# Second norm and router woven into the output products of a decoder step, tile by tile, in one block with the experts; first gather in full fp32 rows

## What is computed

```python
def merge_branches(x, o_a, o_b, g_mrg, w_up_a, w_up_b, w_out):
    g_a, g_b = jnp.split(g_mrg, 2, axis=-1)
    return x + (g_a * (o_a @ w_up_a) + g_b * (o_b @ w_up_b)) @ w_out

def moe_ffn(x, norm_ffn, w_router, b_router, w_gu, b_gu, w_down, b_down):
    xn = rms_norm(x, norm_ffn)
    logits = (xn @ w_router).astype(jnp.float32) + b_router.astype(jnp.float32)
    top_v, top_e = lax.top_k(logits, TOP_K)        # 4 of 32 experts
    gates = jax.nn.softmax(top_v, axis=-1)
    ...
        h = xn[tok] @ w_gu[e] + b_gu[e]
        gate = jnp.minimum(h[:, :D_FF], SWIGLU_LIMIT)
        up = jnp.clip(h[:, D_FF:], -SWIGLU_LIMIT, SWIGLU_LIMIT)
        return ((up + 1.0) * gate * jax.nn.sigmoid(SWIGLU_ALPHA * gate)) @ w_down[e] + b_down[e]
    ...
    return x + out
```

## Time and profile before

| | us |
|---|---|
| median of 3 runs | 1383.79 (1383.48 to 1386.16) |
| the profiled execution | 1390.39 |
| its span, first to last instruction | 1388.6 |
| PE busy | 1255.2 (90%) |
| DVE busy | 355.3 (26%) |
| ACT busy | 218.5 (16%) |
| POOL busy | 24.0 (2%) |
| DMA, mean over the span | 333 GB/s |

### The profile page before, as it was taken

The page is one execution under the profiler, slowest core; times in us unless marked ns, Lnnn a source line. Parts: engine busy times, 40 slices in busy tenths (PEclk is TensorE's granted clock), DMA queues, the critical chain, the costliest instruction groups (busy, mean ns, idle before and its releaser), DMA issues.

```text
span 1388.6 us, 17391 instructions
## 1 busy us (share of the span) xinstructions
PE 1255.2 (90%) x6724; PEld 590.2 (43%) x6724; DVE 355.3 (26%) x905; ACT 218.5 (16%) x476; POOL 24.0 (2%) x26
## 2 busy tenths in 40 slices
PE   6998999999458999999988989889898998989987
PEld 3546678866143343443333323323243333333323
DVE  1551445514254121221211212112121111202113
ACT  2222124410131011011000101001110001010010
POOL 0000000002020000000000000000000000000000
PEclk9999999999757999999999999999999999999999
DMA  9546641487304978999999999999999999999994
GB/s 337 171 119 184 227 152 47 101 278 278 136 4 194 411 292 350 427 429 427 429 428 429 428 429 428 428 429 429 428 428 429 429 428 428 429 429 428 428 429 174
DMA packets 74896, 462.05 MB, mean 333 GB/s; under 512 B 18036, under 2 KB 32996, under 8 KB 50020
## 3 DMA queue, kind: packets, MB, share of 16 engines
q1 hardware_dynamic: 74852, 461.45, 82.1%
HBM read 458.46 MB, written 5.07 MB: 334 GB/s over the span
## 4 chain that ended last, share of the span: by engine, by line
DMA 44%; PE 24%; ACT 1%; DVE 0%; issue 0%; SPq 0%; DVEq 0%; ACTq 0%
DMA arena<-w_down 44%; PE banks L1607 11%; PE banks L1572 9%; PE banks L1553 1%; PE banks L1524 1%; PE banks L1535 0%; PE banks L1563 0%; ACT arena L1633 0%; DVE arena L1958 0%; PE banks L1527 0%; ACT arena L1648 0%; PE banks L1600 0%; PE banks L1585 0%; SPq L424 0%; DVE arena L1685 0%
## 5 line engine op out<-in xcount | busy, mean ns | idle before, releaser
L1572 PE MATMUL banks<-arena 128*64 128x512 f32 x2112 | 472.7, 597 | 37.7 <-DMA arena<-w_gu 37.7
L1572 PEld LDWEIGHTS banks<-arena 128*64 128x64 f32 x2112 | 147.8, 137 | 336.0 <-issue 254.3
L1607 PE MATMUL banks<-arena 128*64 128x512 f32 x1056 | 237.7, 594 | 17.8 <-DMA arena<-w_down 17.8
L1662 DVE TENSOR_SCALAR arena<-banks 128x512 f32<-128x512 f32 x33 | 22.8, 692 | 518.1 <-PE banks L1572 518.1
L1607 PEld LDWEIGHTS banks<-arena 128*64 128x64 f32 x1056 | 72.7, 136 | 164.4 <-issue 118.3
L1637 ACT ACTIVATE arena<-arena 128x512 f32<-128x512 f32 x33 | 20.8, 630 | 559.3 <-DVE arena L1662 559.3
L1685 DVE TENSOR_TENSOR arena<-banks,arena 128x528 f32<-128x528 f32 x68 | 48.1, 708 | 173.6 <-PE banks L1553 173.6
L1143 PE MATMUL banks<-arena 128*128 128x512 f32 (+1 forms) x192 | 80.5, 579 | 0.0
L1553 PE MATMUL banks<-arena 128*128 128x264 f32 x272 | 65.1, 391 | 2.5 <-ACT arena L1648 1.3
L605 PE MATMUL banks<-arena 128*128 128x264 f32 x256 | 62.2, 398 | 0.5 <-ACT arena L832 0.5
L1553 PEld LDWEIGHTS banks<-arena 128*128 128x128 f32 x272 | 50.0, 189 | 23.8 <-issue 12.2
(11 more groups left out here) (330 smaller groups left out, 918.5 us busy)
## 6 DMA issues: line engine op xcount, KB each, us to landing
arena<-w_gu SPq DMA_DIRECT2D x128, 2048.0 KB, 24.9
arena<-w_down SPq DMA_DIRECT2D x64, 2048.0 KB, 25.2
arena<-w_in SPq DMA_DIRECT2D x9, 2048.0 KB, 12.2
arena<-cache_moba_k SPq DMA_DIRECT2D x16, 256.0 KB, 2.8
arena<-cache_moba_v SPq DMA_DIRECT2D x16, 256.0 KB, 2.8
arena<-w_out SPq DMA_DIRECT2D x2, 2048.0 KB, 13.3
arena<-cmp_w_k SPq DMA_DIRECT2D x1, 2048.0 KB, 8.6
arena<-cmp_w_v SPq DMA_DIRECT2D x1, 2048.0 KB, 15.1
```

What stands on the lines that cost most here:

```text
L1572: mm = nc.tensor.matmul(banks[64 * x:64 * x + 64, BG + b, :], xgT[:, c % 4, 64 * (c // 4):64 * (c // 4) + 64], w[:, D * b + 512 * x:D * b ...
L1607: mm = nc.tensor.matmul(banks[64 * x:64 * x + 64, BY, :], aT[:, c, 64 * part:64 * part + 64], w[:, 512 * x:512 * x + 512], start=False, st ...
L1662: nc.vector.tensor_scalar(gate, banks[:, BG, :], LIMIT, None, ALU.min).then_inc(S["clip"], 1)
```

## The change

1. The blocks of the norm and of the router are gone; all of it stands in the dense block, and the experts' programs follow in the same block with no barrier (`experts_sp`, `experts_pe`, `experts_act`, `experts_dve`, otherwise the old code).
2. `route_pe`, `route_act` and `route_dve` take the place of the output products' code. The sample rows come first, then four half tiles of 512 columns. Once a half tile is added, its rows are transposed as they are, not normed. The gain is folded into w_router (one multiplication, with the gain loaded one element per row), and the factor 1/rms is applied to the logits. The second half of tile 1 is interrupted half way by the router products of tile 0.
3. Root by tile; the scaled rows are made on ScalarE beside this. The bias splits stand between VectorE's additions. w_router, b_router and the two forms of the gain are loaded behind the first expert's slots 0 and 1. Slots 3 and 5 wait for `out_done` 5.
4. `gather_first`: the first pass gathers from the fp32 rows themselves, 3 tiles by 2 halves, and doesn't wait for the three parts. The parts are made later: ScalarE casts, VectorE subtracts (`less`), POOL no longer.
5. The list products and the turn of the table stand inside gate_up of pass 0, after a quarter, a half and three quarters (`lists`). VectorE does the softmax weights, both `less`, `lists` and the table by expert before the clip of pass 0; before, `lists` came after its product.

```diff
+            sp.dma_start(gain2, t["norm_ffn"].partition_broadcast(P)).then_inc(r_in, 16)
+            sp.dma_start(w_router, t["w_router"].rearrange("(c p) n -> p c n", p=P)).then_inc(r_in, 16)
+            sp.dma_start(b_router, t["b_router"].partition_broadcast(P)).then_inc(r_in, 16)
+            with nc.allow_non_contiguous_dma("one gain per row of the router's weights"):
+                sp.dma_start(gainT, t["norm_ffn"].rearrange("(c p) -> p c", p=P)).then_inc(r_in, 16)
...
-            sp.wait_ge(out_done, 3)
+            sp.wait_ge(out_done, 5)
...
+            pe.wait_ge(S["sel"], 1)
+            pe.wait_ge(r_scaled, NT)
+            for i in range(NT):
+                r = ROWS[i]
+                for x in range(2):
+                    mm = nc.tensor.matmul(banks[64 * x:64 * x + 64, BX, :], sel_rows[0:r, i, :], xn2[0:r, i, 512 * x:512 * x + 512],
+                                          start=(i == 0), stop=(i == NT - 1), tile_position=(0, 64 * x))
+            mm.then_inc(S["gathered"], 1)
...
+            def turn_h(i, chunks, bank, done, turn):
+                r = ROWS[i]
+                pe.wait_ge(h_done, done)
+                for k, c in enumerate(chunks):
+                    mm = nc.tensor.transpose(banks[:, bank, r * k:r * k + r], h[0:r, i, P * c:P * c + P], ident[0:r, 0:r])
+                mm.then_inc(h_turned, 1)
...
+            def route(i, bank, chunks, kept):
+                r = ROWS[i]
+                pe.wait_ge(h_kept, kept)
+                for c in chunks:
+                    mm = nc.tensor.matmul(banks[0:r, bank, 0:NEXP], hT[:, c, P * i:P * i + r], w_router[:, c, :], start=(c == 0), stop=(c == KC - 1))
...
+            out_half(0, 0)
+            turn_h(2, range(KC), 5, 1, 1)
+            out_half(0, 1)
+            out_half(1, 0)
+            turn_h(0, range(4), 6, 2, 2)
+            turn_h(0, range(4, KC), 7, 3, 3)
+            pe.wait_ge(r_folded, 1)
+            route(2, 4, range(KC), 1)
+            turn_h(1, range(4), 5, 4, 4)
+            out_half(1, 1, lambda: route(0, 6, range(KC), 3))
+            route(1, 7, range(4), 4)
+            turn_h(1, range(4, KC), 0, 5, 5)
+            route(1, 7, range(4, KC), 5)
+            pe.wait_ge(r_chosen, 3)
...
+            square(3, 1, slice(512, D), 5)
+            act.wait_ge(r_mean, 1)
+            root(1, 3, h_mean)
+            keep_turned(1, range(4, KC), 0, 5)
+            scale(1, 3)
+            act.wait_ge(r_shifted, 1)
+            nc.scalar.activation(exps, exps, ACT.Exp).then_inc(r_exp, 1)
+            act.wait_ge(r_scaled, 3)
+            nc.scalar.copy(x_parts[:, 1, 0, :], xn2[:, 1, :]).then_inc(r_cast, 1)
...
+                dve.wait_ge(r_logits, k)
+                settle(nc.vector.scalar_tensor_tensor(logits[0:r, i, :], banks[0:r, bank, 0:NEXP], h_inv[0:r, i:i + 1], b_router[0:r, :], ALU.mult, ALU.add))
+                settle(nc.vector.max(top8[0:r, i, :], logits[0:r, i, :]))
+                settle(nc.vector.max_index(top_i[0:r, i, :], top8[0:r, i, :], logits[0:r, i, :]))
+                settle(nc.vector.tensor_copy(top_f[0:r, i, :], top_i[0:r, i, :]))
+                settle(nc.vector.tensor_tensor(hits[0:r], const("iota")[0:r, 0:NEXP].unsqueeze(1).broadcast_to([r, TOPK, NEXP]),
+                                               top_f[0:r, i, 0:TOPK].unsqueeze(2).broadcast_to([r, TOPK, NEXP]), ALU.is_equal))
+                nc.vector.tensor_reduce(chosen[0:r, i, :], hits[0:r].rearrange("p k e -> p e k"), X, ALU.add).then_inc(r_chosen, 1)
...
+            dve.wait_ge(r_in, 64)
+            nc.vector.tensor_tensor(w_router, w_router, gainT.unsqueeze(2).broadcast_to([P, KC, NEXP]), ALU.mult).then_inc(r_folded, 1)
             dve.wait_ge(h_in, 32)
+            dve.wait_ge(out_done, 1)
...
+            split_bias(0)
+            add_out(0, 0, 2)
+            dve.wait_ge(r_clear, 4)
+            gained(2, slice(0, D), 1).then_inc(r_gained, 1)
+            split_bias(1)
+            add_out(0, 1, 3)
+            invert(2, 1)
+            gained(0, slice(0, D), 3).then_inc(r_gained, 1)
+            invert(0, 2)
+            add_out(1, 0, 4)
+            dve.wait_ge(r_sq, 3)
+            nc.vector.tensor_scalar(h_mean, h_ss[:, 2:3], 1.0 / D, EPS, ALU.mult, ALU.add).then_inc(r_mean, 1)
+            choose(2, 4, 1)
+            gained(1, slice(0, 512), 4)
+            choose(0, 6, 2)
+            add_out(1, 1, 5)
+            gained(1, slice(512, D), 5).then_inc(r_gained, 1)
+            invert(1, 3)
+            choose(1, 7, 3)
+            nc.vector.tensor_tensor(exps, logits, top8[:, :, 0:1].broadcast_to([P, NT, NEXP]), ALU.subtract).then_inc(r_shifted, 1)
+            flat = rank.rearrange("p a b -> p (a b)")
+            dve.wait_ge(r_ranked, 1)
+            settle(nc.vector.scalar_tensor_tensor(flat, banks[:, 1, 0:NT * NEXP], 1.0, chosen.rearrange("p a b -> p (a b)"), ALU.add, ALU.mult))
+            settle(nc.vector.tensor_scalar(flat, flat, -1.0, None, ALU.add))
...
+            def lists(c):
+                if c == 1:
+                    pe.wait_ge(l_wanted, 1)
+                    nc.tensor.matmul(banks[:, 7, 0:1], const("before"), over[:, 1:2], start=True, stop=True).then_inc(l_found, 1)
+                if c == 3:
+                    pe.wait_ge(l_wanted, 2)
+                    nc.tensor.matmul(banks[:, 7, 1:2], const("before"), over[:, 3:4], start=True, stop=True)
+                    nc.tensor.matmul(banks[:, 7, 2:3], const("over_expert"), over[:, 2:3], start=True, stop=True)
+                    nc.tensor.matmul(banks[:, 7, 3:4], ones, over[:, 2:3], start=True, stop=True)
+                    nc.tensor.matmul(banks[:, 7, 4:5], ones, over[:, 3:4], start=True, stop=True).then_inc(l_found, 1)
+                if c == 5:
...
+                    mm.then_inc(l_turned, 1)
+
+            gather_first(pe)
+            pe.wait_ge(r_counted, 1)
+            for i in range(NT):
+                mm = nc.tensor.matmul(banks[:, 7, 0:1], many[:, i, :], ones[:, 0:1], start=(i == 0), stop=(i == NT - 1))
+            mm.then_inc(r_ranked, 1)
+            turn_rows(pe, 0)
+            gate_up(pe, 0, 0, 0, None, lists)
+            gather(pe, 1)
+            turn_rows(pe, 1)
+            turn_product(pe, 0)
...
+                last = nc.vector.tensor_scalar(sel_rows[0:r, i, :], const("iota")[0:r, 0:CAP], rank[0:r, i, 0:1], None, ALU.is_equal)
+            last.then_inc(S["sel"], 1)
...
+            dve.wait_ge(S["gathered"], 1)
+            select(lambda i: rank[:, i, 1:2])
+            dve.wait_ge(r_ranked, 2)
...
+            def less(q):
+                for i in range(2):
+                    dve.wait_ge(r_cast, 2 * q + i + 1)
+                    nc.vector.tensor_tensor(xn2[:, i, :], xn2[:, i, :], x_parts[:, i, q, :], ALU.subtract).then_inc(r_left, 1)
...
+            less(0)
+            dve.wait_ge(l_found, 1)
+            settle(nc.vector.tensor_scalar(over[:, 2:3], banks[:, 7, 0:1], 0.0, over[:, 1:2], ALU.is_equal, ALU.mult))
+            nc.vector.tensor_tensor(over[:, 3:4], over[:, 0:1], over[:, 2:3], ALU.subtract).then_inc(l_wanted, 1)
+            dve.wait_ge(r_exp, 1)
+            settle(nc.vector.tensor_tensor(exps, exps, chosen, ALU.mult))
...
+            last.then_inc(l_tripled, 1)
+            less(1)
+            lists()
+            dve.wait_ge(l_turned, 1)
...
+            clip_product(dve, 0)
+            product(dve, 0)
+            step(1, 1, 0)
```

1371 lines of the change are left out of this document (662 added, 709 removed).

## The result

| | before | after |
|---|---|---|
| median, us | 1384.12 (1383.48 to 1386.16, 4 runs) | 1348.62 (1346.76 to 1353.21, 4 runs) |
| ratio, 95% interval | | 0.9746 [0.9719, 0.9773] |
| the profiled execution, us | 1390.39 | 1346.76 |
| from the start of the output work to the second pass's products, us | 119.3 | 77.6 |
| from there to the end of the span, us | 939.3 | 941.3 |

Faster by 35.5 us between the medians, 43.6 between the two profiled executions; the prediction was 42, at 1341.8 with a range of 1333 to 1351. The last two lines are what the prediction reckoned with, read from the starts of two groups of TensorE in the timeline (449.26 - 330.00 before, 403.62 - 326.00 after; the chain puts the products' start 0.17 us later in both kernels, at 449.43 and 403.79).

What follows compares the result with a forecast made beforehand. TensorE's serial work before the second pass's products bounded the start, delaying the saturated transfers behind it; its terms moved those products from 449.43 to 407.5, and 42 us off the median 1383.79 gave 1341.8 us, range 1333 to 1351.

Steps and rivals of the forecast that it cites:

- The path: Output work's start at 330.00 to second pass's products: these come at 407.5 instead of 449.43, 42 us earlier.
- the four loads: Small loads SP issues ahead of h: cost nothing; 10 us longer would make the first transposes wait 3 to 4 us.
- VectorE's chain behind the first list product: First pass, ahead of the clip: 14.1 us of VectorE work until 404.6, 2.7 us after TensorE is done.
- the 4.3: Between passes 0 and 1: old 5.3 us from products' end to next products, without 1.0 us of list products.
- the forecast's case: Serial routing tail: TensorE at half clock, 1.2 GHz, gain 38 to 45 us; chance 0.60.
- Rival 1: Serial routing tail: the clock stays up at 2.4 GHz, gain 49 us (range 46 to 50), time 1335; chance 0.16.
- The rise inside the gather: First gather: its 12 dense instructions could restore full clock before the expert's products, 2 to 3 us more gain.
- Rival 2: New routing order: a VectorE chain or late load holds TensorE; gain 32 to 34 us, time 1350; chance 0.16 (30 to 37).
- Rival 3: Routing pieces still begin only after the last output product; gain about 18 us, time 1366; chance 0.04.
- Rival 4: First expert passes: clock does not rise, each costs 20 us more, four give 1422; chance 0.02, with anything eating all.
- the last one: Whole-kernel sum: runs' median 1383.79 lies 6.6 below the profiled execution; the same 42 us off gives 1341.8.

Runs made afterwards that it cites:

- ladder of kernels: Kernel before, The kernel with late loads, norm late, turns behind, changed kernel: output work to second pass's products 119.3, 115.2, 97.7, 85.7, 77.6 us.
- the fillers: Changed kernel plus four fp32 products of 512 columns that nobody reads, in TensorE's waits in the routing tail; ratio 0.9674, median 1341.23 us.
- norm late: turns behind, plus VectorE's first addition waiting until all four half tiles of the output product are done; ratio 0.9874.
- turns behind: Changed kernel with TensorE doing all four half tiles of output products before the transposes and router products; ratio 0.9782.
- second profile: Changed kernel, no edit, run and profiled once more; ratio 0.9719, median 1346.5 us.
- The kernel with late loads: norm late, plus SP issuing the four small router loads behind slots 3 and 5, after the output products; ratio 1.0000, 1386.0 us beside 1385.89.

## Why the prediction was right, and where it was not

**Where the gain came from.** The ladder of kernels splits the path's 119.3 - 77.6 = 41.7 us: 17.5 from the early loads (115.2 to 97.7), 12.0 from the norm beside the output products (97.7 to 85.7, of which 6.8 are bias splits that would else be in the way), 8.1 from queues that don't wait on turns done late (85.7 to 77.6), 4.1 for all the rest (119.3 to 115.2), the fp32 gather and the block edges with it. The gather alone is worth 3.6 in the changed kernel. The clock's 2 us in the kernel with 97.7 count for the loads and against the norm: without them it would be some 15.6 and 14. And these are prices in this order of steps. Late loads with the norm beside the output products, and early loads in the kernel before, were not run.

**The path: right.** I had 77.5 us from the start of the output work (407.5 - 330.0); it was 77.6 by the timeline and 77.8 by the chain, from which the forecast was made. Counted from that start by the forecast's own terms: last output product ends at 35.6, measured 35.9; first gather 45.0, measured 45.4; first gate and up products 53.5, measured 54.8; pass 0's last product 71.9, measured 72.8; second pass's products 77.5, measured 77.6. The DMA waits and the four loads were costed at nothing, and nothing in the products waits for them; the margin was small, though. The last of the four landed at about 322.5 (318.13 + 4.4), and VectorE's multiplication with the gain stood at 325.87.

**Terms that were off, and cancelled.** The gather took 5.58 us, not 5.1. I had no term for the six count products of L1500 behind it (1.44 us). From the end of the gather to the first gate and up products it was 3.9 us instead of 3.4, since ScalarE's copy of the gathered rows runs beside them; with the 0.4 us at the gather's start and its own 0.5 that makes the 1.3 us at the first products. VectorE's chain behind the first list product was 14.1 us in the forecast and ran from 386.08 to 399.62, 13.5 us; it began 0.4 us earlier than I had it, counted from the start, and the products ended 0.9 us later; so the clip was 0.9 us late, not 2.7. After the clip I took 1.4 us off the 4.3 because the gather runs in that time; from the clip to the second pass's products it was 4.0 (399.62 to 403.62). That way leads over VectorE's four operations of clip and product and the turn behind them, and not over the gather. So the four errors are +1.3 up to the first products, -0.4 in them, -1.8 at the clip and +1.1 behind it. Each has its reason, but that they cancel to 0.1 or 0.3 us is luck.

**The clock: right in the forecast's case.** I chose half clock for the tail and it was 0.52 from 370 to 384. Rival 1's 7 us for a clock that stays up were measured with the fillers as 6.3. The rise inside the gather, which I had put at 2 to 3 us, did not come in the changed kernel; it came with the norm late, where it was worth 2.0.

**Rival 2** (a chain of waits, or a late load) was not seen in the change, but is real: a queue in the wrong order costs 8.1 us, a late load 17.5. **Rival 3** had 18 us if the routing came behind the output products; measured 21.6 with the norm behind them too, and 33.6 with only the turns behind. **Rival 4** fell: the clock was 1.00 from 384 to 390, and the picture has 9 in every slice behind. In the second profile it dipped once more in the second pass and cost 1.7 us.

**The failed step is the last one:** "the runs' median, 1383.79, lies 6.6 lower, and I take the same 42 off". The measured median is 6.8 above the forecast. The profile of the kernel before was one with a low clock in the dense layer (0.89 from 160 to 220), and that of the change was the fastest of its runs; the path says nothing of either. On the medians the gain was 35.5 us in the first comparison and 39.1 in the second (1385.59 to 1346.5), against 41.7 on the path and 41.6 between the second pair of profiles (1386.57 and 1345.01). A part of the rest can be named. The changed kernel lost 2.0 us after the path in both its profiles, in two ways that another execution of the same kernel did not show: the last transposes' start in the first profile and in the second:

```profile
1337.72 2.84 PE L1559 MATMUL banks<-arena 128*128 128x128 f32 x24 [2.79 <-issue]
```

```profile
1335.87 2.84 PE L1559 MATMUL banks<-arena 128*128 128x128 f32 x24 [0.80 <-DVE arena L1247]
```

and in the second profile the second pass's products at a lower clock, 15.60 us instead of 13.90, 1.7 of the 2.0 us:

```profile
398.00:404.00 6.00, 4.51 (x26) 2.11 (x22) 3.16 (x8) 2.27 (x4) 0.00 (x0) 0.85 1.02 436
404.00:410.00 6.00, 6.00 (x26) 1.87 (x24) 0.00 (x0) 0.00 (x0) 0.00 (x0) 0.87 0.54 167
```

The path's gain minus these 2 us is 39.7. Why the first comparison's medians show only 35.5 stays open; its four runs of the changed kernel spread over 6.5 us. It is not only that spread: in all ten comparisons with an edit or the change the medians gain less than the path, by 1.5 to 5.9 us (the path of before taken as 119.0), and the stretch behind the path is longer by 0 to 2.7 us. The kernel with late loads lost its 3.8 us wholly. The path's gain is thus too high a forecast for the median here, and what takes the rest is not shown.

## What to carry to other kernels

Read a step that you move as a set of queues: the gain did not come from TensorE's new order, and 8.1 us of it were lost as soon as ScalarE's order no longer matched TensorE's. Before a serial stage is rebuilt, look for its small loads; to issue these four behind the output products cost 17.5 us here, some 2 of them by the clock. What their early issue alone would give the kernel before was not tried. And take a forecast's base from a stretch that the change touches, then put the gain on the median with the spread of whole runs in the range, since one profile can differ by some us in code that nobody changed.

## What the hardware showed that I had not expected

The granted clock in the dense layer differs from execution to execution (0.77 to 0.97 from 160 to 220), and moves everything behind by up to 10 us. It can dip once more in the second expert pass (15.49 and 15.60 us for products of 13.90, in two of the ten profiles of the changed kernel and what was made of it), and I found no rule for when. In two kernels with the same instructions on TensorE the half clock ended inside the first gather (4.68 us, norm late) or only behind it (5.58 us, load late).

Four filler products with no reader, 512 columns each, stood in waits of TensorE's and so delayed nothing that I can see; they took some 4 us there and gave 6.3 back.

The issue of the router's bias, a load of 16 KB that goes to all partitions, held SP's queue for 17.14 us in the changed kernel and for 8.90 with the loads late, where most of its neighbours took 0.3 to 0.5 us and the same load took 0.43 us in the kernel before. It cost nothing in the changed kernel, since x, issued behind it at 318.61, was wanted only after 329, and about 1 us at most with the loads late. What holds it was not tried.
